# Output norm, recurrence projection and gate tiles placed among the heads of the attentions; selection in four parts

## What is computed

```python
# first block, each layer
y = recurrence(...)                                   # 8 heads of 64
y = ((y - mean) * rsqrt(var + LNX_EPS)) * lnx_g + lnx_b
y_a = ((y + bonus) * gate) @ rwkv_out
y_b = mla_attention(q_a, kv_a, k_rope) @ mla_out      # 8 heads
x = x + gate * ((sigmoid(g_a) * y_a + sigmoid(g_b) * y_b) @ w_o)
# second block, each layer
aq, ak, av, iq, ik, iw, bq, bk, bv, gates = split(rms_norm(x) @ w_in)
# rms_norm by head and rotation of aq, ak, ik, bq, bk
ya = attention over the 64 keys of best score         # A: 8 heads; score from iq, ik, iw
yb = diff_attention(bq, bk, bv, lam)                  # B: 4 heads, two softmaxes each
yb = rms_norm(yb) * (1 - lam_init)
g_a, g_b = split(sigmoid(gates + gate_bias))
x = x + (g_a * (ya @ w_up_a) + g_b * (yb @ w_up_b)) @ w_out
```

## Time and profile before

| | |
|---|---|
| median of three runs | 3532.3 us (3531.6 to 3533.58) |
| profiled execution | 3528.04 us |
| its span, first to last instruction | 3526.3 us |
| mean granted clock of TensorE | 0.963 |
| PE busy | 3321.3 us, 94% |
| DVE busy | 863.2 us, 24% |
| ACT busy | 459.7 us, 13% |
| DMA, mean over the span | 192 GB/s, 678.10 MB |

### The profile page before, as it was taken

One profiled execution on the slowest core, in us unless ns is written; L12 is line 12 of the kernel. 1 busy time (PEld: TensorE's weight loads), 2 busy tenths in 40 slices (PEclk: granted clock), 3 DMA queues, 4 the chain that ended last, 5 costly groups with the idle time before them and its releaser, 6 DMA issues.

```text
span 3526.3 us, 47602 instructions
## 1 busy us (share of the span) xinstructions
PE 3321.3 (94%) x21128; PEld 2528.8 (72%) x21128; DVE 863.2 (24%) x1661; ACT 459.7 (13%) x1054; POOL 35.6 (1%) x74
## 2 busy tenths in 40 slices
PE   6998899989888999999999999998989999988999
PEld 4775688878565666666666777776866888876888
DVE  3523300152333111111111111112463101463100
ACT  2221200222221000000000000001221001122000
POOL 4000000000000000000000000000000000000000
PEclk9999999999889999999999999999988999997999
DMA  8464244444204888999999988981422343432342
GB/s 283 149 221 142 84 131 153 136 150 134 84 12 155 298 293 292 299 321 345 353 352 358 312 299 298 298 286 57 126 84 96 126 160 123 131 108 69 127 151 96
DMA packets 538365, 678.10 MB, mean 192 GB/s; under 512 B 14346, under 2 KB 487584, under 8 KB 538032
## 3 DMA queue, kind: packets, MB, share of 16 engines
q1 hardware_dynamic: 534320, 670.11, 58.0%
q10 hardware_dynamic: 1440, 3.67, 0.3%
q0 software_dynamic: 2400, 1.26, 0.1%
HBM read 673.95 MB, written 1.05 MB: 191 GB/s over the span
## 4 chain that ended last, share of the span: by engine, by line
PE 91%; DVE 4%; ACT 2%; issue 1%; DMA 1%; SPq 0%; ACTq 0%; DVEq 0%
PE bank L471 62%; PE accum L471 28%; DVE w L1621 1%; DMA ring<-in_ada_w_dram 1%; DVE w L1607 1%; DVE w L1613 1%; PE bank L562 1%; PE bank L694 1%; ACT w L1268 0%; ACT w L1214 0%; ACT L1214 0%; DVE sh L1621 0%; SPq L2217 0%; DVE w L1610 0%; ACT h L1214 0%
## 5 line engine op out<-in xcount | busy, mean ns | idle before, releaser
L471 PE MATMUL bank<-h,ring 128*128 128x256 f32 (+1 forms) x3712 | 816.9, 383 | 28.0 <-DVE h L1613 12.2
L471 PEld LDWEIGHTS bank<-h,ring 128*128 128x128 f32 (+1 forms) x3712 | 705.1, 191 | 137.1 <-issue 33.8
L471 PE MATMUL bank<-w,ring 128*128 128x256 f32 (+1 forms) x2816 | 572.0, 364 | 8.3 <-DVE w L1607 7.4
L471 PEld LDWEIGHTS bank<-w,ring 128*128 128x128 f32 x2816 | 510.6, 191 | 62.1 <-issue 6.3
L471 PE MATMUL bank<-ring,w 128*32 128x256 f32 (+1 forms) x4928 | 496.2, 380 | 0.0
L471 PEld LDWEIGHTS bank<-ring,w 128*32 128x32 f32 (+1 forms) x4928 | 366.1, 132 | 112.1 <-issue 7.8
L471 PE MATMUL accum<-ring,qa 128*32 128x512 f32 (+1 forms) x1232 | 253.0, 595 | 0.0
L1607 DVE TENSOR_TENSOR sg<-bank,sg 128x256 f32<-128x256 f32 (+1 forms) x126 | 51.6, 409 | 774.3 <-ACT sg L1214 774.3
L471 PE MATMUL accum<-w,ring 128*128 128x256 f32 x1056 | 233.1, 379 | 0.0
L471 PE MATMUL bank<-w 64*64 64x64 f32 (+4 forms) x3072 | 171.4, 247 | 58.4 <-ACT w L1268 33.2
L471 PEld LDWEIGHTS accum<-w,ring 128*128 128x128 f32 x1056 | 200.8, 190 | 27.1
(11 more groups left out here) (251 smaller groups left out, 1864.7 us busy)
## 6 DMA issues: line engine op xcount, KB each, us to landing
ring<-in_moe_w_dram SPq DMA_DIRECT2D x378, 1024.0 KB, 6.6
ring<-in_w_in_dram SPq DMA_DIRECT2D x76, 1024.0 KB, 5.3
ring<-in_ada_w_dram SPq DMA_DIRECT2D x48, 1024.0 KB, 9.0
ring<-in_w_ffn_in_dram SPq DMA_DIRECT2D x44, 1024.0 KB, 5.2
ring<-in_ffn_w_dram SPq DMA_DIRECT2D x33, 1024.0 KB, 5.3
ring<-in_w_ffn_out_dram SPq DMA_DIRECT2D x22, 1024.0 KB, 5.1
ring<-in_w_o_dram SPq DMA_DIRECT2D x8, 1024.0 KB, 5.2
ring<-in_w_out_dram SPq DMA_DIRECT2D x8, 1024.0 KB, 5.2
```

Of the source, the lines that this page charges most:

```text
L471: ins = nc.tensor.matmul(o, lhsT, rhs, start=start, stop=stop, skip_group_check=skip)
```

## The change

Four things are done, in both layers of each block.

- `root_by_log` takes the place of `root` and `inverse_root` for kk, for the output norm, for the five groups of heads and for B's norm: Ln on ACT, and then Exp with scale -0.5, also on ACT. `root` stays elsewhere.
- First block: the eight turned queries and the rotated key stand directly behind the queries. The output norm on DVE moves behind heads 0 and 1 of mla, and the eight tiles of ya stand between the transposes and the weighted sum of heads 2 to 7 (`YA_AT`). A buffer of the attention (pT1) moves to another place.
- Second block: the sixteen gate tiles leave the projection and stand in B and A (`GATES_AT`), ACT copies them with their bias by Identity and takes four Sigmoids of 1024 columns at the end of A (`gates_open`). The sums and roots of B's norm stand in A, its scaling behind head 4 of A. ub comes before ua.
- The sums and rotations of the groups stand at other tiles u, and the selection is cut into four parts, one behind each of the groups 1 to 4.

```diff
+YA_AT = [[], [], [0], [1], [2], [3], [4, 5], [6, 7]]
+GATES_AT = {"B": [[0, 1], [2, 3], [4], [5, 6], [7]], "A": [[8], [9], [10], [11], [12], [13], [14], [15], []]}
...
-        sm1, pb1, pT1 = (slot4(i)[:, 0:768].rearrange("p (b n) -> p b n", b=2) for i in (9, 10, 11))
+        sm1, pb1, pT1 = (slot4(i)[:, 0:768].rearrange("p (b n) -> p b n", b=2) for i in (9, 10, 1))
...
                 scores(1)
+                if beside:
+                    beside(-1)
...
                     ins.then_inc(f, 1)
+                    if beside:
+                        beside(hd)
...
+            def project_tile(tag, kt, src, at, held):
+                m = at % (16 // kt)
+                if m == 0:
+                    held[:] = piece(kt)
+                s, w = held
+                t, f = take(tag + (at,))
+                contract(t[:, 0:T], kt, lambda k: w(k, m * P, m * P + P), lambda k: src[:, k, :]).then_inc(f, 1)
+                if m == 16 // kt - 1:
+                    release.append(s)
...
-                    if hd == 4:
+                    if hd == 6:
                         pe.wait_ge(squared, next_of("squared"))
                         sums(("yvar", l), blk, 4, ysq, take_upper)
-                    turned_query(hd - 4)
                 release.append(s)
+                for hd in range(8):
+                    turned_query(hd)
+                t, f = take(("krot", l))
+                mm(t[0:96, 0:T], c("rot96")[0:96, :], qa[0:96, 5, :], last=True).then_inc(f, 1)
...
-                    if i < 4:
-                        turned_query(4 + i)
...
-                t, f = take(("krot", l))
-                mm(t[0:96, 0:T], c("rot96")[0:96, :], qa[0:96, 5, :], last=True).then_inc(f, 1)
                 if l == 0:
                     mod_columns(1, 0)
-                pe.wait_ge(yg_ready, next_of("yg_ready"))
-                project(("ya", l), 4, yT)
+                held = []
+                def out_tiles(hd):
+                    if hd < 0:
+                        return
+                    if hd == 2:
+                        pe.wait_ge(yg_ready, next_of("yg_ready"))
+                    for at in YA_AT[hd]:
+                        project_tile(("ya", l), 4, yT, at, held)
...
-                    if u == 3:
+                    if u == 5:
                         head_sums(0)
                     elif u == 7:
                         head_turns(0)
...
                         head_sums(1)
                     elif u == 10:
                         index_scores()
+                    elif u == 12:
+                        head_turns(1)
                     elif u == 13:
                         head_sums(2)
-                    elif u == 14:
-                        head_turns(1)
+                    elif u == 17:
+                        head_turns(2)
                     elif u == 18:
                         head_sums(3)
-                    elif u == 20:
-                        head_turns(2)
-                    elif u == 24:
+                    elif u == 21:
+                        head_turns(3)
+                    elif u == 22:
                         head_sums(4)
-                    elif u == 26:
-                        head_turns(3)
-                    elif u == 32:
+                    elif u == 25:
                         head_turns(4)
...
+                def gate_tiles(tag, hd):
+                    for m in GATES_AT[tag][hd + 1]:
+                        if m % 2 == 0:
+                            held[:] = piece(8, 256)
+                        s, w = held
+                        t, f = take(("gt", l, m))
+                        lo = m % 2 * P
+                        contract(t[:, 0:T], KD, lambda k: w(k, lo, lo + P), lambda k: h[:, k, :]).then_inc(f, 1)
+                        if m % 2:
+                            release.append(s)
+                def beside_b(hd):
+                    gate_tiles("B", hd)
+                def beside_a(hd):
+                    gate_tiles("A", hd)
+                    if hd == 0:
+                        pe.wait_ge(squared, next_of("squared"))
+                        sums(("yb2", l), ones[:, :], 4, sq2, take_beside)
...
-                pe.wait_ge(squared, next_of("squared"))
-                sums(("yb2", l), ones[:, :], 4, sq)
+                          lambda hd, kt: avn[:, kt, hd * 64:hd * 64 + 64], side, take_beside, beside_a)
+                pe.wait_ge(ysub, next_of("ysub"))
+                project(("ub", l), 4, oB2)
                 pe.wait_ge(*read_out(("A", l, "o", 7)))
                 project(("ua", l), 4, oA2)
-                pe.wait_ge(ysub, next_of("ysub"))
-                project(("ub", l), 4, oB2)
                 pe.wait_ge(merged, next_of("merged"))
...
+            def root_by_log(keys, buf, n, eps):
+                at = 0
+                for key, w in keys:
+                    act.wait_ge(*full(key))
+                    fn(buf[:, at:at + w, :], psum_of(key)[:, 0:w * T].rearrange("p (j t) -> p j t", t=T), ACT.Ln,
+                       scale=1.0 / n, bias=c("eps", eps, eps + 1)).then_inc(reader_of(key), 1)
+                    at += w
+                for key, _ in keys:
+                    act.wait_ge(*read_out(key))
+                fn(buf[:, 0:at, :], buf[:, 0:at, :], ACT.Exp, scale=-0.5).then_inc(rooted, one("rooted"))
...
+                    if beside:
+                        beside(hd)
                     if hd:
                         turned(tag, hd - 1)
                     if hd > 1:
                         weighted_sum(tag, hd - 2)
+                if beside:
+                    beside(n)
                 turned(tag, n - 1)
                 weighted_sum(tag, n - 2)
+                if beside:
+                    beside(n + 1)
                 weighted_sum(tag, n - 1)
...
-                        root([(("kk", l, 0), 2), (("kk", l, 1), 2)], rsk, 1, 2)
+                        root_by_log([(("kk", l, 0), 2), (("kk", l, 1), 2)], rsk, 1, 2)
...
-                    if hd == 5:
-                        root([(("yvar", l, 0), 2), (("yvar", l, 1), 2)], rsy, 64, 1)
+                    if hd == 7:
+                        root_by_log([(("yvar", l, 0), 2), (("yvar", l, 1), 2)], rsy, 64, 1)
...
+                def gate_copies(tag, hd):
+                    for m in GATES_AT[tag][hd + 1]:
+                        act.wait_ge(*full(("gt", l, m)))
+                        fn(sg[:, m, :], psum_of(("gt", l, m))[:, 0:T], ACT.Identity, bias=col2(l, "gate_bias", m)
+                           ).then_inc(reader_of(("gt", l, m)), 1)
+                def beside_b(hd):
+                    if hd != 1:
+                        gate_copies("B", hd - 2 if hd else -1)
+                def beside_a(hd):
+                    if hd != 1:
+                        gate_copies("A", hd - 2 if hd else -1)
+                    if hd == 3:
+                        root_by_log([(("yb2", l, 0), 2), (("yb2", l, 1), 2)], rs2, P, 0)
+                    elif hd == 9:
+                        for m in range(12, 16):
+                            act.wait_ge(*read_out(("gt", l, m)))
+                        for q in (2, 3, 0, 1):
+                            fn(sg[:, 4 * q:4 * q + 4, :], sg[:, 4 * q:4 * q + 4, :], ACT.Sigmoid
+                               ).then_inc(gates_open, one("gates_open"))
...
+                attention(("B", l), beside_b)
+                act.wait_ge(*read_out(("B", l, "o", 2)))
+                act.wait_ge(*read_out(("B", l, "o", 3)))
+                fn(sq2[:, :, :], oB2[:, :, :], ACT.Square).then_inc(squared, one("squared"))
+                attention(("A", l), beside_a)
...
-                inverse_root([("kk", l, 0), ("kk", l, 1)], rsk, 4)
+                dve.wait_ge(rooted, next_of("rooted"))
...
+                def beside_head(hd):
+                    if hd == 0:
+                        dve.wait_ge(rooted, next_of("rooted"))
+                        tt(yT[:, :, :], yT[:, :, :], rsy[:, 0:4, :], MUL).then_inc(dve_step, 1)
+                        dve.wait_ge(dve_step, stepped())
+                        for j in range(RJ):
+                            ins = ts(yT[:, j, :], yT[:, j, :], col1(l, "lnx_g", j), col1(l, "lnx_b", j))
+                        ins.then_inc(dve_step, 1)
+                        dve.wait_ge(dve_step, stepped())
+                    elif hd == 1:
+                        dve.wait_ge(*read_out(("bonus", l, 1)))
+                        tt(yT[:, :, :], yT[:, :, :], bon[:, :, :], ADD).then_inc(dve_step, 1)
+                        dve.wait_ge(dve_step, stepped())
+                        dve.wait_ge(*read_out(("g", l, 3)))
+                        tt(yT[:, :, :], yT[:, :, :], gat[:, :, :], MUL).then_inc(yg_ready, one("yg_ready"))
+                    else:
+                        gated_tiles(YA_AT[hd - 1])
+                attention(("mla", l), None, beside_head)
+                gated_tiles(YA_AT[7])
...
+                def selection(part):
+                    if part == 1:
```

(34 more changed lines are left out.)

154 lines of the change are left out of this document (62 added, 92 removed).

## The result

The kernel after takes 3406.7 us (median of 4 runs, 3404.3 to 3415.4) against 3532.0 us before: the ratio is 0.9649, 95% interval 0.9631 to 0.9667, 125 us less. The forecast was 3424, range 3396 to 3450. The profiled execution of after is the slowest of its four, 3415.4 us (span 3413.6); against the profiled one of before that is 112.7 us less.

What follows compares the result with a forecast made beforehand. PE (TensorE) bounds the kernel, busy 3321 of 3526 us, so only its idle time and lower clock can be won. Gains 74.7 + 1 + 32.0 + 1 = 108.7, say 108 us, off median 3532.3: 3424 us, range 3396 to 3450.

Steps and rivals of the forecast that it cites:

- Gate tiles beside the heads: Second block's attentions and branches: gate tiles fill PE's waits, clock stays 1.00; 60.5 for 97.5 and 98.2, 74.7 us saved.
- Switching: Second block's attentions: PE going to and from 16 gate tiles costs 0.1 us each, 1.6 us.
- Roots by logarithm: All changed roots: Ln and Exp on ACT replace DVE's 6.55 us reciprocal; 0.5 us a layer at kk, together 1 us.
- Selection in four parts: Second block, DVE: parts between group turns stay covered by PE's tiles; 0, slack 1.4 to 4 us.
- End of B's norm and the gates: Second block, end of attentions: norm's tail goes beside A's heads, four sigmoids (5.5 us with load) stay covered; 0.
- Queries to values: First block: 31.4 us in place of 47.2 and 47.6, saving 15.8 + 16.2 = 32.0 us.
- the new wait at the key tile: First block, fourth key tile: PE waits about 2.7 us for the key turn's bank, which DVE reads late.
- Projection beside mla: First block: about 41.1 us against 42.1 and 41.2, first heads leaving the clock at 0.50; 1 us saved.
- Heads in series: Rival, second block: 24 heads still pay 0.67 and some 1.3 us each, 48 us, time 3472; chance 0.11.
- Gates at half clock: Rival, second block's attentions: gate tiles run at 0.50, 170 us longer in all, time 3594; chance 0.02.
- The change holding PE up by what it sheds: Rival, second block: selection or early groups delay PE ahead of B, 24.5 us a layer, time 3473; chance 0.04.
- Less stands in the way: Rival: switching free, bank wait hidden, mla at full clock; 12 + 5 + 7 us more, 3400; chance 0.09.

Runs made afterwards that it cites:

- e3: Kernel after with all sixteen gate tiles of the second block back ahead of the attentions, B's norm left beside A's heads: 3490.8 us (one run).
- e5: Kernel after with both score products of each B head on rows 0 to 63 instead of different halves: 3419.6 us (one run).
- e1: Kernel after with the first head group's sums back behind its third tile, between the narrow index products: 3410.6 us, ratio 0.9656.
- e9: Kernel before with only the roots' form changed to logarithm and exponential on ACT, all at their old places: 3529.3 us (10 runs), ratio 0.9994.
- e6: Kernel after with square root on ACT and reciprocal on DVE at all the roots' new places: 3437.7 us (one run).
- e4: Kernel after with all four parts of the selection behind the last rotated group on DVE: 3444.5 us (one run).
- e2: Kernel after with the product that turns the shared key moved behind the key and value tiles: 3408.5 us, ratio 0.9646.
- e7: Kernel after with the first block's output norm right behind the key rotation on DVE and a-branch tiles from before mla's first head: 3392.3 us, ratio 0.9611.
- e8: Kernel after with A's scores two heads at a time and key tiles of two heads in halves of one bank: 3398.9 us, ratio 0.9626.
- e10: Kernel after with first sums moved back, norm in DVE's gap with earlier a-branch tiles, paired A scores and paired key tiles: 3382.3 us (5 runs), ratio 0.9577.
- e11: Kernel of e10 with gate tiles spread anew, so that A's last head has one too: 3380.2 us, ratio 0.9576.

## Why the prediction was right

**Gate tiles beside the heads.** Right in mechanism and near in size. The stretch was to take 115.8 us (60.5 + 55.3) and took 110.2; in all 41.9 + 37.8 = 79.7 us were saved where 74.7 were forecast. e3 shows that it is the gate tiles: without them the rest is worth 2.6 us in layer 0. Terms that were mis-sized: B's heads were counted at 2.67 and take 1.94 us, since the "one more pair of score products" costs nothing beside the first when they use different row halves (e5: 0.64 us for 8 records); that is 2.9 us. The Trainium skill's page "TensorE: Matmul & The Clock Gate" (Part 3: Packing small matmuls — row/col tiling) says that small products placed on different tiles of the array run concurrently; its figures are for tiles of 32 rows or columns, some 4 ns for each further one. The rows here agree for halves of 64 rows (8 records 0.93 us, 4 records 0.92), and the forecast should have weighed it. Switching, 1.6, hardly shows: A's heads come to 16.3 us besides tiles, sums and waits, where 16.2 were counted without it. The root, 1 us, shows 0.46; the 1 us for what I didn't see was not needed. These make some 6 where 5.6 is to be explained; the two branch projections take 27.9 us, 27.6 were counted. The last head's 0.65 is there (0.67). On the other side, the projection ahead was counted at 116.3 us (171.6 less 55.3) and took 117.1 and 121.8. 1.7 and 3.4 us are the clock dip that the move of the first sums caused (without it, in e1, layer 0 takes 115.4); and layer 1 began at a lower clock (13.75 us for its first 64 records, 10.75 in before). In layer 1 of all other runs these records take 12.2 to 13.7 us, in e9 too (12.15), which has before's order, and in e6 (12.17), which has before's roots. So neither alone makes it, and its cause is open.

**Roots by logarithm.** A root is 4.99 us on ACT in e3 (two loads of 1.28, two Ln 1.27 together, one Exp 1.06), 4.8 were counted; when nothing covers it, PE's wait for the copy behind it grows by 4.15. The Trainium skill's page "ScalarE: Activation LUTs" (What ACT_TABLE_LOAD costs) gives each switch some 1380 ns of drain besides the load; by an estimate from that figure the root would be 2.8 us longer. The trace disagrees: the next activation starts 0.01 us after a load's end, and all gaps in the root together are 0.1 us. The 1 us for the form of the roots was costed too narrowly, though, at kk alone, where e6 finds nothing. In its new places the form is worth 31 us (e6), and at its old places it gives nothing (e9), because what DVE sheds ACT takes on, in front of copies that PE waits for. I had not looked at what queues behind the root on ACT in the head groups; the answer happened to be mild, since the change moves those roots as well.

**Selection in four parts.** The zero was right, and its cover was needed, for more than I put on it: 5.8 us a layer was the price of part 4 alone; all four parts in one piece cost 16.0 (e4), a quarter of it as clock behind the waits.

**End of B's norm and the gates.** No wait for the opened gates or the b branch shows: zero, as counted. The wait ahead of the merged tiles is 0.98 us, as before.

**First block.** Queries to values: 31.9 and 33.6 us where 31.4 was forecast; the new wait at the key tile is 2.33 and 2.32 us where about 2.7 was. In layer 1 the clock fell behind it (20 records 6.22 us, 4.53 in layer 0), which I had not counted. That this wait costs 5 us in both layers together held in size: e2 moves it and gets back 1.9 and 3.0. It held not as counted, since PE then waits 2.3 and 2.6 us at the first scores instead, and gains in the waits and the clock behind. Projection beside mla: 38.9 and 38.8 us where 41.1 was forecast, the half clock at the first heads is there, and together the block saved 34.6 us in place of 33.0. That this sum is so near is in part luck: queries to values came out 0.5 and 2.2 us longer than counted, mla 2.2 and 2.3 shorter. What I took for given there, the idle first heads, was a choice of place: e7 wins 7.9 and 9.5 us by putting the same norm into a gap of DVE's queue that I had not looked for.

**The rivals.** Heads in series: none but two of the twelve heads show a wait. Gates at half clock: the stretch is at 1.00. The change holding PE up by what it sheds: no wait at any turn or at B's first scores. "Less stands in the way" is the one that was half true, by the size of B's heads and of switching; its bank wait was not hidden, and mla did fall to half clock. For the profiled execution 3420 was forecast and 3415.4 came: the second block gave 5.0 more and the first 1.6, kk's 1 did not show and 1.6 was lost elsewhere. Both lie between the b branch of layer 0 and the queries of layer 1 of the first block, 521.2 us in after and 518.5 in before; e2 and e4, which do not differ there, take 516.8 and 521.4, so this is what single executions differ by. The other 13 of the 17 us between 3424 and the median of 3406.7 come from the profiled executions themselves: that of before lay 4 under its median, that of after 9 above its own. This was not traced to a place.

## What to carry to other kernels

Where heads of attention are a chain over three engines, put independent matrix tiles between transposes and weighted sum and ahead of the first head; the idle time comes back and the clock with it, here 21 us of idle time and some 18 us of clock, 39 a layer. Before such a move, take the long items out of the queues that it leans on (a reciprocal, a selection), and check the queue that takes them on. Then read the new trace for gaps and halves left: 24 us more came from there.

## What the hardware showed that was not expected

- Products that use 64 rows, or 64 output columns, overlap when neighbours use different halves: 8 records in 0.93 us and 1.57 in the same half (e5); 24 records of 64 columns in 2.81 us where 12 took 2.80 (e8).
- 32 records of 4 columns back to back, with PE busy all the time, were followed by a granted clock of 0.66 in a 5 us window (after, layer 0). They cost 1.7 us in most layers, 3.3 to 3.4 in the two whose 64 records ahead took 13.7 us, and nothing in one; with four records of 512 columns between them the tiles behind ran at their full-clock time in all six layers (e1, e10, e11). What makes the clock fall there is open.
- A wait of 1.4 us more cost 4.6 us in all, as the clock fell behind it (e9), while a wait of 2.3 us moved behind the value tiles, at the same length, gave 1.9 and 3.0 us (e2): its length alone does not price a short wait.
